# The first two weight chunks in quarters, interleaved on TensorE, and the squares of x moved from GpSimd to ScalarE and VectorE

## The chip, the cores and the metric

The kernel runs on one core of a Trainium2 chip. The metric is the device time of one launch in microseconds (us). All weights are streamed from the chip's main memory (HBM) in each launch.

## What is computed

One layer of a hybrid encoder in float32: 16 meta tokens and 256 frames (272 token columns), model width 2048. Only the front of it matters here:

```python
u = rmsnorm(h, norm_mix_g)                 # y = x * rsqrt(mean(x*x) + eps) * g
proj = u @ w_in                            # one combined input projection
rq, rk, rv, rg, cq, ckv, kr = jnp.split(proj, IN_SPLITS, axis=-1)
c_kv = rmsnorm(ckv, kv_norm_g)             # 256 wide
c_q = rmsnorm(cq, q_norm_g)                # 512 wide
# retention heads and latent attention, then
h = h + jnp.concatenate([ret_out, mla_out], axis=-1) @ w_o
h = h + jnp.square(jax.nn.relu(rmsnorm(h, norm_mlp_g) @ w_up)) @ w_down
return rmsnorm(h[frames], final_norm_g)
```

The kernel multiplies the projection weights with x times its gain first, and applies the row factor rsqrt(mean(x*x) + eps) to the results later. So the sum of squares of x is not needed by the first multiplications, but by what follows them.

## The kernel before, in words

**Layout.** Activations are transposed: 128 features on the partitions, tokens in the free dimension. x is `x_in`, 16 tiles (index k) of 128x272. Weights come in chunks: a chunk `c` is 128 output columns of a weight matrix with all 2048 input rows, stored as 128x2048 (16 tiles of 128x128, 1024 KB). Chunks 0 and 1 are the 256 columns of `ckv`, chunks 2 to 5 are `cq`, chunk 6 the rotary key, then come the heads' chunks.

**Split operands.** TensorE multiplies in a rounded float32 format (`fp32r`). To keep float32 precision each operand is split into a rounded part and a rest. For a chunk, ScalarE copies `raw` into `hi` (`split_hi`, L548, in two halves of 128x1024), and VectorE subtracts, `lo = raw - hi` (`split_lo`, L830). For x, ScalarE writes `xs[:, k, 0:TOK]`, x times gain rounded (`x_round`, L589), and VectorE writes the rest `xs[:, k, TOK:]` (`x_rest`, L843), one instruction for each of the 16 tiles on each engine. `narrow` (L323) then makes three matmuls of 272 columns for each k (lo with x, hi with the rest of x, hi with x); `wide` (L291) makes two for each k (512 and 256 columns).

**Buffers.** There are four `raw` buffers, but two of `hi`, two of `lo` and two result banks `acc`, all indexed by c % 2. A chunk's half of `hi` can be written only when the chunk two before has used that half (`chunk_used`), a chunk's matmuls can begin only when the result of the chunk two before has been read out of its bank (`acc_read`), and a load into `raw` waits until VectorE has made `lo` from it (`lo_ready`).

**Order of work.** Every engine runs its own list of instructions strictly in the order in which the code writes them, with semaphores between the engines. The start is:

- SyncE's queue (L243 to L256) issues the gains, half of chunk 0, x tiles 0 to 3, x tiles 4 to 7, the other half of chunk 0, x tiles 8 to 11 and 12 to 15, chunks 1 and 2, the constants, chunk 3, and then the stream of chunks.
- ScalarE (L584 to L605): first half of chunk 0, x tiles 0 to 7, second half of chunk 0, x tiles 8 to 15, chunk 1, chunks 2 and 3, then `kv_sq`, the squares of `ckv`.
- VectorE (L849 to L867) follows with the rests in the same order; after the splits of chunk 2 it reads the result of chunk 0 (`ckv[:, 0]`, L864), after those of chunk 3 the result of chunk 1.
- GpSimd (L1205 to L1214) waits for all of x, squares it in one instruction (`x_sq = x_in * x_in`, 128x4352) and folds the 16 tiles in halves, 8, 4, 2 and 1 tiles, counting on `ssx`.
- TensorE (L426 to L436): `narrow(0)`, tile by tile as `x_lo` allows, `narrow(1)`, `wide(2)`, `wide(3)`, then a multiplication with ones that adds the squares over the partitions (`ps_x`, L432; waits for `ssx` 5), the same for `ckv` (`ps_v`), then chunks 4, 5, 6 and the heads.

Of the kernel before, what the change touches and what calls it, by code (L numbers as in the profile page):

```python
# [13 lines left out]
P = 128  # L26
# [39 lines left out]


# [27 lines left out]
side_landed first_half gains_landed consts_landed table_in""".split()  # L95


def hymba_block(nc, w_in, w_side, w_o, w_up, w_down, x_all, x_frames, gains_in, consts_in, out):
    ctx = ExitStack()
    with ctx:  # L100
        sem = {n: ctx.enter_context(nc.semaphore(n)) for n in EVENTS}
        raw_landed = [ctx.enter_context(nc.semaphore(f"raw_landed{i}")) for i in range(RAWS)]
        x_part = [ctx.enter_context(nc.semaphore(f"x_part{i}")) for i in range(4)]
# [133 lines left out]
        def _(sp):  # L237
# [49 lines left out]
        def _(pe):  # L287
# [34 lines left out]

            def narrow(c, more=0, ready=None):  # L323
                a = acc[c % 2][:, 0:TOK]
                for k in range(KT):
                    if k % 8 == 0:
                        pe.wait_ge(sem["lo_ready"], 2 * c + k // 8 + 1 + 2 * more)
                    if k == 0 and c >= 2:
# [3 lines left out]
                    wh = hi[c % 2][:, k * P:k * P + P]  # L332
                    wl = lo[c % 2][:, k * P:k * P + P]
                    mm(a, wl, xs[:, k, 0:TOK], k == 0, False)
                    mm(a, wh, xs[:, k, TOK:], False, False)
                    m = mm(a, wh, xs[:, k, 0:TOK], False, k == KT - 1)
                    if k % 8 == 7:
                        m.then_inc(sem["chunk_used"], 1)

# [83 lines left out]
            def x_parts(k):  # L423
                pe.wait_ge(sem["x_lo"], k + 1)

            narrow(0, ready=x_parts)  # L426
            narrow(1)
# [3 lines left out]
            pe.wait_ge(sem["ssx"], 5)  # L431
# [112 lines left out]
        def _(act):  # L544
# [3 lines left out]
            def split_hi(c, part, more=0):  # L548

                if c < 0 or c >= C_END:  # L550
                    return
                if c == 0 and part == 0:
                    act.wait_ge(sem["first_half"], 16)
                elif part == 0 or c == 0:
                    act.wait_ge(raw_landed[c % RAWS], 16 * (c // RAWS + 1) + 4 * more)
                if c >= 2:
                    act.wait_ge(sem["chunk_used"], 2 * (c - 2) + part + 1 + 2 * more)
# [25 lines left out]

            act.wait_ge(sem["meta_pad"], 2)  # L584
            copy(cen[:], pt_m[:]).then_inc(sem["table_in"], 1)
            split_hi(0, 0)
            act.wait_ge(sem["gains_landed"], 16)

            def x_round(k):  # L589
                act.wait_ge(x_part[k // 4], 16)  # L590
                act.activation(xs[:, k, 0:TOK], x_in[:, k, :], ACT.Identity, scale=gain(G_MIX + k)).then_inc(sem["x_hi"], 1)  # L591

            for k in range(8):
                x_round(k)
            split_hi(0, 1)
            for k in range(8, 16):
                x_round(k)
            split_hi(1, 0)
            split_hi(1, 1)

            for c in range(2):
                split_hi(c + 2, 0)
                split_hi(c + 2, 1)
# [222 lines left out]
        def _(dve):  # L826
# [22 lines left out]
            split_lo(0, 0)  # L849
            dve.wait_ge(sem["gains_landed"], 16)  # L850
            for k in range(8):
                if k % 4 == 0:
                    dve.wait_ge(x_part[k // 4], 16)
                x_rest(k)
            split_lo(0, 1)
            for k in range(8, 16):
                x_rest(k)
            split_lo(1, 0)
            split_lo(1, 1)
            for c in range(2):  # L860
                split_lo(c + 2, 0)
                split_lo(c + 2, 1)
                dve.wait_ge(sem["chunk_used"], 2 * c + 2)
                dve.tensor_copy(ckv[:, c, :], acc[c % 2][:, 0:TOK]).then_inc(sem["acc_read"], 1)  # L864

# [329 lines left out]
        def _(pool):  # L1195
# [213 lines left out]
```

## Time and profile before

| | us |
|---|---|
| median of 3 runs | 1194.45 (1194.44 to 1195.57) |
| span of the profiled execution, first to last instruction | 1192.3 |
| TensorE busy (matmul) | 1152.4 (97%) |
| VectorE busy | 736.5 (62%) |
| ScalarE busy | 609.2 (51%) |
| GpSimd busy | 154.3 (13%) |
| mean granted TensorE clock | 0.986 of full speed |

The profiled execution gives no time of its own besides its span; the median of the runs lies 2.15 us above that span, which is what lies around the first and the last instruction. The engines are called PE (TensorE's matmuls), PEld (its weight loads), DVE (VectorE), ACT (ScalarE), POOL (GpSimd) and SP (SyncE); a "q" behind a name is the engine's sequencer, which issues DMAs. "L591" is line 591 of the kernel. All positions are us from the span's start. The busy shares are averages over 1192 us; the span in 40 slices shows TensorE at 2 tenths in the first slice, at 9 in nearly all others, and at 5 in the last one.

### The profile page before, as it was taken

The numbers are of one execution on the slowest core, as the hardware profiler recorded it, in microseconds if no ns is written. First come the engines' busy times: TensorE is split into PE (matmuls) and PEld (weight loads), VectorE is DVE, ScalarE is ACT, GpSimd is POOL, SyncE is SP. The second block draws the span as 40 slices with busy tenths as digits, with TensorE's granted clock in tenths as the row PEclk, the third lists the DMA queues.
The fourth block names the chain that finished last, engine by engine and source line by source line (L and its number), as shares of the span: only waits on it lengthen the run. The fifth ranks groups of instructions, "written<-read, shape, count | busy, mean of one in ns | idle before, by whom it ended". The sixth has DMA issues, their size and how long they took to land.

```text
span 1192.3 us, 18902 instructions
## 1 busy us (share of the span) xinstructions
PE 1152.4 (97%) x6758; PEld 1004.7 (84%) x6758; DVE 736.5 (62%) x962; ACT 609.2 (51%) x942; POOL 154.3 (13%) x167
## 2 busy tenths in 40 slices
PE   2999999999998999999999999999999999999995
PEld 2897898888887888888888888888888888888884
DVE  7786767677768667666665444445666665444443
ACT  4454565555556556555554444444555554444441
POOL 5011111111113331000000111111000000111111
PEclk7999999999999999999999999999999999999997
DMA  7443433333415554554555555455455445544531
GB/s 295 183 163 133 168 133 132 132 145 128 167 71 216 190 193 176 187 200 177 182 201 180 177 199 187 176 184 198 183 177 200 185 177 189 198 176 180 204 109 70
DMA packets 29260, 206.33 MB, mean 173 GB/s; under 512 B 3376, under 2 KB 3376, under 8 KB 5680
## 3 DMA queue, kind: packets, MB, share of 16 engines
q1 hardware_dynamic: 28080, 199.66, 46.4%
q10 hardware_dynamic: 1152, 6.29, 1.4%
q8 instruction: 18, 0.29, 0.1%
q14 instruction: 10, 0.08, 0.0%
HBM read 203.84 MB, written 2.10 MB: 173 GB/s over the span
## 4 chain that ended last, share of the span: by engine, by line
PE 95%; DVE 3%; ACT 1%; DMA 1%; issue 0%; DVEq 0%; SPq 0%; ACTq 0%
PE acc L289 86%; PE ps_qn L289 3%; PE ps_qr L289 2%; DVE xs L845 1%; PE ps_y L289 1%; PE ps_v L289 1%; PE ps_x L289 1%; PE ps_kn L289 1%; DMA x_in<-x_all 1%; DVE res L828 0%; DVE lo L828 0%; ACT xs L591 0%; DVE hid L1089 0%; DVE mla_o L828 0%; ACT hi L546 0%
## 5 line engine op out<-in xcount | busy, mean ns | idle before, releaser
L828 DVE TENSOR_TENSOR lo<-raw,hi 128x1024 fp32r<-128x1024 f32 x366 | 450.3, 1231 | 245.0 <-ACT hi L546 240.7
L289 PE MATMUL acc<-xs,hi 128*128 128x512 f32 (+1 forms) x1952 | 589.3, 365 | 0.0
L546 ACT ACTIVATE hi<-raw 128x1024 fp32r<-128x1024 f32 x366 | 386.6, 1057 | 234.5 <-PE acc L289 228.4
L289 PE MATMUL acc<-xs,lo 128*128 128x256 f32 (+1 forms) x1648 | 457.9, 286 | 22.2 <-DVE xs L845 22.2
L289 PE MATMUL acc<-hid,hi 128*128 128x512 f32 x1280 | 450.8, 400 | 3.2 <-DVE hid L1089 3.2
L289 PEld LDWEIGHTS acc<-xs,hi 128*128 128x128 f32 x1952 | 346.7, 190 | 51.6
L289 PE MATMUL acc<-hid,lo 128*128 128x256 f32 x1280 | 352.3, 281 | 0.0
L289 PEld LDWEIGHTS acc<-xs,lo 128*128 128x128 f32 x1648 | 312.3, 190 | 31.3 <-DVE lo L828 9.1
L289 PEld LDWEIGHTS acc<-hid,hi 128*128 128x128 f32 x1280 | 238.1, 189 | 59.5 <-DVE hid L1089 4.5
L289 PEld LDWEIGHTS acc<-hid,lo 128*128 128x128 f32 x1280 | 242.5, 189 | 4.7
L546 ACT ACTIVATE half_b<-acc 128x256 f32<-128x256 f32 x132 | 50.7, 384 | 216.7 <-PE acc L289 216.7
L1197 POOL TENSOR_TENSOR t<-half_b,res 128x256 f32<-128x256 f32 x47 | 34.7, 739 | 658.1 <-ACT half_b L546 650.3
L828 DVE TENSOR_TENSOR res<-acc,t 128x256 f32 (+1 forms) x47 | 20.0, 425 | 90.6 <-POOL t L1197 90.6
L828 DVE TENSOR_TENSOR z<-acc,half_b 128x256 f32<-128x256 f32 x64 | 27.2, 425 | 54.6 <-ACT half_b L546 54.6
L1197 POOL TENSOR_TENSOR sum_sq<-sum_sq,sq 128x256 f32<-128x256 f32 x47 | 51.8, 1102 | 56.1 <-ACT sq L810 36.8
L1148 DVE SCALAR_TENSOR_TENSOR r<-z,rstd 128x256 f32<-128x256 f32 x64 | 27.3, 426 | 2.2
L788 ACT ACTIVATE sq<-r 128x256 f32<-128x256 f32 x64 | 26.8, 418 | 3.3 <-DVE r L1148 3.1
L828 DVE TENSOR_TENSOR hid<-sq,hid 128x256 f32 (+1 forms) x64 | 26.9, 420 | 0.0
L789 ACT ACTIVATE hid<-r 128x256 f32 (+1 forms) x64 | 25.7, 402 | 0.0
L810 ACT ACTIVATE sq<-res 128x256 f32 (+1 forms) x32 | 13.5, 421 | 21.1 <-DVE res L828 21.1
L845 DVE SCALAR_TENSOR_TENSOR xs<-x_in,gains,xs 128x272 fp32r<-128x272 f32 x16 | 22.3, 1464 | 0.2 <-ACT xs L591 0.2
L1197 POOL TENSOR_TENSOR rk<-zk,consts 128x272 f32<-128x272 f32 x8 | 8.3, 1034 | 65.9 <-ACT swk L546 65.9
(175 smaller groups left out, 621.0 us busy)
## 6 DMA issues: line engine op xcount, KB each, us to landing
raw<-w_up SPq DMA_DIRECT2D x64, 1024.0 KB, 4.8
raw<-w_down SPq DMA_DIRECT2D x64, 1024.0 KB, 4.8
raw<-w_in SPq DMA_DIRECT2D x38, 1024.0 KB, 4.8
raw<-w_o SPq DMA_DIRECT2D x16, 1024.0 KB, 4.8
side<-w_side ACTq DMA_DIRECT2D x8, 768.0 KB, 5.8
x_in<-x_all SPq DMA_DIRECT2D x4, 544.0 KB, 7.7
res<-x_frames SPq DMA_DIRECT2D x1, 2048.0 KB, 7.6
out<-res SPq DMA_DIRECT2D x2, 640.0 KB, 3.0
```

Source lines behind the costliest of these rows:

```text
L289: return pe.matmul(o, l, m, start=start, stop=stop)
L546: return act.activation(o, i, ACT.Copy)
L788: act.activation(sq[:], r[:], ACT.Square).then_inc(sem["up_sq"], 1)
L789: act.activation(hid[:, n, 0:FRAMES], r[:], ACT.Square).then_inc(sem["up_hi"], 1)
L810: act.activation(sq[:], res[:, n, :], ACT.Square).then_inc(sem["dn_sq"], 1)
L828: return dve.tensor_tensor(o, a, b, op)
L845: dve.scalar_tensor_tensor(out=xs[:, k, TOK:], in0=x_in[:, k, :], scalar=gain(G_MIX + k), in1=xs[:, k, 0:TOK].bitcast(F32), op0=ALU.mult, ...
L1148: dve.scalar_tensor_tensor(out=r[:], in0=z[:], scalar=0.0, in1=rstd[:], op0=ALU.max, op1=ALU.mult).then_inc(sem["up_r"], 1)
L1197: return pool.tensor_tensor(o, a, b, op)
```

## The change

- SyncE's queue: the first two chunks come as quarter, quarter, half, and x in five parts (tiles 0-1, 2-3, 4-7, 8-11, 12-15), interleaved. The gains go through ScalarE's queue. The constants are issued after chunk 3 and no longer before it.
- ScalarE and VectorE split in the order in which the pieces come. ScalarE then also squares x, in four instructions of four tiles (128x1088), two after the first half of chunk 2 and two after its second half.
- VectorE folds the squares (8, 4, 2, 1 tiles: 2176, 1088, 544 and 272 columns) between the splits of chunk 3 and the reads of `ckv`. GpSimd does neither.
- TensorE multiplies tiles 0-3 of chunk 0, tiles 0-3 of chunk 1, tiles 4-7 of chunk 0, tiles 4-7 of chunk 1, then the second half of chunk 0 and that of chunk 1. The number of matmuls is the same.

```diff
+X_PARTS = ((0, 2), (2, 4), (4, 8), (8, 12), (12, 16))
+QUARTER = W // 4
@@ block.sync
-            sp.dma_start(gains[:], gains_in).then_inc(sem["gains_landed"], 16)
-            sp.dma_start(raw[0][:, 0:W // 2], w_in[0, :, 0:W // 2]).then_inc(sem["first_half"], 16)
-            sp.dma_start(x_in[:, 0:4, :], x_all[:, 0:4, :]).then_inc(x_part[0], 16)
-            sp.dma_start(x_in[:, 4:8, :], x_all[:, 4:8, :]).then_inc(x_part[1], 16)
-            sp.dma_start(raw[0][:, W // 2:], w_in[0, :, W // 2:]).then_inc(raw_landed[0], 16)
-            for n in range(2, 4):
-                sp.dma_start(x_in[:, 4 * n:4 * n + 4, :], x_all[:, 4 * n:4 * n + 4, :]).then_inc(x_part[n], 16)
-            load(w_in[1], 1)
+            piece(0, 0, 1, sem["w_0a"])      # columns [a, b) * QUARTER of chunk c
+            x_load(0)
+            x_load(1)
+            piece(1, 0, 1, sem["w_1a"])
+            piece(0, 1, 2, sem["w_0b"])
+            x_load(2)
+            piece(1, 1, 2, sem["w_1b"])
+            x_load(3)
+            piece(0, 2, 4, raw_landed[0])
+            x_load(4)
+            piece(1, 2, 4, raw_landed[1])
             load(w_in[2], 2)
+            load(w_in[3], 3)
             sp.dma_start(consts[:], consts_in).then_inc(sem["consts_landed"], 16)
-            load(w_in[3], 3)
@@ block.tensor
+            def first_pair():
+                for part in range(2):
+                    for c in range(2):
+                        pe.wait_ge(sem["part_lo"], 2 * part + c + 1)
+                        for k in range(4 * part, 4 * part + 4):
+                            if c == 0:
+                                pe.wait_ge(sem["x_lo"], k + 1)
+                            m = narrow_step(c, k)
+                        if part == 1 and c == 0:
+                            m.then_inc(sem["chunk_used"], 1)
+                for c in range(2):
+                    pe.wait_ge(sem["lo_ready"], 2 * c + 2)
+                    for k in range(8, KT):
+                        if c == 0:
+                            pe.wait_ge(sem["x_lo"], k + 1)
+                        m = narrow_step(c, k)
+                        if c == 1 and k == 8:
+                            m.then_inc(sem["chunk_used"], 1)
+                    m.then_inc(sem["chunk_used"], 1)
-            narrow(0, ready=x_parts)
-            narrow(1)
+            first_pair()
             wide(2, 2, x_wide, x_hi)
             wide(3, 3, x_wide, x_hi)
             pe.wait_ge(sem["consts_landed"], 16)
-            pe.wait_ge(sem["ssx"], 5)
+            pe.wait_ge(sem["ssx"], 8)
@@ block.scalar
+            act.dma_start(gains[:], gains_in).then_inc(sem["gains_landed"], 16)
+            def x_square(n):
+                act.activation(x_sq[:, 4 * n:4 * n + 4, :], x_in[:, 4 * n:4 * n + 4, :],
+                               ACT.Square).then_inc(sem["ssx"], 1)
+            piece_hi(0, 0, 1, sem["w_0a"]).then_inc(sem["part_hi"], 1)
             act.wait_ge(sem["gains_landed"], 16)
+            x_round(0)
+            x_round(1)
+            piece_hi(1, 0, 1, sem["w_1a"]).then_inc(sem["part_hi"], 1)
+            piece_hi(0, 1, 2, sem["w_0b"]).then_inc(sem["part_hi"], 1)
+            x_round(2)
+            piece_hi(1, 1, 2, sem["w_1b"]).then_inc(sem["part_hi"], 1)
+            x_round(3)
+            piece_hi(0, 2, 4, raw_landed[0]).then_inc(sem["hi_ready"], 2)
+            x_round(4)
+            piece_hi(1, 2, 4, raw_landed[1]).then_inc(sem["hi_ready"], 2)
+
+            split_hi(2, 0)
+            x_square(0)
+            x_square(1)
+            split_hi(2, 1)
+            x_square(2)
+            x_square(3)
+            split_hi(3, 0)
+            split_hi(3, 1)
             act.wait_ge(sem["acc_read"], C_CQ)
             act.activation(kv_sq[:], ckv[:], ACT.Square).then_inc(sem["kv_sq"], 1)
@@ block.vector
+            def x_sum(n, step):
+                dve.wait_ge(sem["ssx"], step)
+                tt(x_sq[:, 0:n, :], x_sq[:, 0:n, :], x_sq[:, n:2 * n, :], ALU.add).then_inc(sem["ssx"], 1)
+            def kv_read(c):
                 dve.wait_ge(sem["chunk_used"], 2 * c + 2)
                 dve.tensor_copy(ckv[:, c, :], acc[c % 2][:, 0:TOK]).then_inc(sem["acc_read"], 1)
...
+            piece_lo(0, 2, 4, "hi_ready", 2).then_inc(sem["lo_ready"], 2)
+            x_rests(4)
+            piece_lo(1, 2, 4, "hi_ready", 4).then_inc(sem["lo_ready"], 2)
+
+            split_lo(2, 0)
+            split_lo(2, 1)
+            kv_read(0)
+            x_sum(8, 4)
+            split_lo(3, 0)
+            split_lo(3, 1)
+            x_sum(4, 5)
+            kv_read(1)
+            x_sum(2, 6)
+            x_sum(1, 7)
@@ block.gpsimd
-            for n in range(4):
-                pool.wait_ge(x_part[n], 16)
-            tt(x_sq[:], x_in[:], x_in[:], ALU.mult).then_inc(sem["ssx"], 1)
-            n = KT // 2
-            step = 1
-            while n:
-                pool.wait_ge(sem["ssx"], step)
-                tt(x_sq[:, 0:n, :], x_sq[:, 0:n, :], x_sq[:, n:2 * n, :], ALU.add).then_inc(sem["ssx"], 1)
-                n //= 2
-                step += 1
```

The rests on VectorE before `piece_lo(0, 2, 4, ...)` follow the pieces of ScalarE one by one. `narrow_step(c, k)` is the body of the loop of `narrow`.

## Rows read from the trace of the kernel before

**Rows 1.** Chain that ended last, in order of time: start us, us, engine, what.

```profile
13.44 16.68 DVE xs L845 x4
...
30.17 14.93 PE acc L289 x93
```

**Rows 2.** Waits in the first 35 us: who waited for whom, us, times, longest.

```profile
PE acc L289 <- DVE xs L845: 22.2, 5, 9.2
```

**Rows 3.** Timeline of VectorE, 8 to 33 us: start us, us, instruction, count.

```profile
8.51 3.39 DVE L845 SCALAR_TENSOR_TENSOR xs<-x_in,gains,xs 128x272 fp32r<-128x272 f32 x8 [0.18 <-ACT xs L591]
...
13.36 7.68 DVE L845 SCALAR_TENSOR_TENSOR xs<-x_in,gains,xs 128x272 fp32r<-128x272 f32 x1
...
13.36 18.91 DVE L845 SCALAR_TENSOR_TENSOR xs<-x_in,gains,xs 128x272 fp32r<-128x272 f32 x8
```

**Rows 4.** Timeline of GpSimd, 13 to 33 us.

```profile
13.24 7.50 POOL L1197 TENSOR_TENSOR x_sq<-x_in 128x4352 f32<-128x4352 f32 x1 [11.55 <-DMA x_in<-x_all]
20.82 9.92 POOL L1197 TENSOR_TENSOR x_sq<-x_sq 128x2176 f32<-128x2176 f32 x4
```

**Rows 5.** Whole core, stretches: PE, PEld, DVE, ACT, POOL busy; PEclk, DMA share, GB/s.

```profile
26.00:33.00 7.00, 4.92 (x17) 4.09 (x18) 7.00 (x7) 0.00 (x0) 4.58 (x3) 0.50 0.00 0
...
368.00:370.00 2.00, 1.97 (x5) 1.54 (x6) 2.00 (x6) 1.36 (x2) 0.00 (x0) 0.50 0.98 418
```

**Rows 6.** Timeline of TensorE from 39 to 52 us: first matmul of chunk 2, the square sums.

```profile
39.92 0.28 PE L289 MATMUL acc<-xs,lo 128*128 128x256 f32 x1
...
50.90 0.62 PE L289 MATMUL ps_x<-x_sq,consts 128*128 128x272 f32 x2
```

**Rows 7.** Timeline: where ScalarE and GpSimd begin on what has landed.

```profile
6.02 1.06 ACT L546 ACTIVATE hi<-raw 128x1024 fp32r<-128x1024 f32 x1 [3.56 <-DMA raw<-w_in]
...
7.83 3.41 ACT L591 ACTIVATE xs<-x_in,gains 128x272 fp32r<-128x272 f32 x8 [0.76 <-DMA x_in<-x_all]
...
15.60 2.00 ACT L546 ACTIVATE hi<-raw 128x1024 fp32r<-128x1024 f32 x2
18.09 1.06 ACT L546 ACTIVATE hi<-raw 128x1024 fp32r<-128x1024 f32 x1 [0.49 <-DMA raw<-w_in]
```

**Rows 8.** Stretches of SyncE: us, PEclk, DMA share, GB/s.

```profile
3.00:4.00 1.00, 1.00 0.99 193
...
14.00:16.00 2.00, 1.00 1.02 426
```

**Rows 9.** DMA issues in the first 35 us: what, KB each, median us to landing.

```profile
x_in<-x_all SPq DMA_DIRECT2D x4, 544.0 KB, 7.7
...
gains<-gains_in SPq DMA_DIRECT2D x1, 35.0 KB, 1.9
```

**Rows 10.** ScalarE's squares of ckv, from the timeline.

```profile
42.58 0.66 ACT L605 ACTIVATE kv_sq<-ckv 128x544 f32<-128x544 f32 x1 [1.64 <-DVE ckv L864]
```

**Rows 11.** VectorE's groups by form, 35 to 110 us: count, busy us, mean ns, idle before.

```profile
L828 DVE TENSOR_TENSOR lo<-raw,hi 128x1024 fp32r<-128x1024 f32 x22 | 26.8, 1221 | 6.4 <-ACT hi L546 6.4
L828 DVE TENSOR_TENSOR side_lo<-side,side_hi 128x1280 fp32r<-128x1280 f32 x2 | 3.0, 1492 | 3.4 <-ACT side_hi L546 3.4
L864 DVE COPY ckv<-acc 128x272 f32<-128x272 f32 x2 | 0.9, 434 | 0.0
```

**Rows 12.** TensorE alone, stretches: us, busy, PEclk, DMA share, GB/s.

```profile
14.05:21.20 7.15, 0.01 (x1) 0.65 1.01 421
...
33.30:50.90 17.60, 17.60 (x116) 1.00 0.56 209
```

**Rows 13.** Timeline of TensorE: first matmul of neighbouring k-steps of chunk 0, at two rates.

```profile
9.97 0.43 PE L289 MATMUL acc<-xs,lo 128*128 128x272 f32 x1
...
10.65 0.43 PE L289 MATMUL acc<-xs,lo 128*128 128x272 f32 x1
...
33.30 0.29 PE L289 MATMUL acc<-xs,lo 128*128 128x272 f32 x1
...
33.67 0.29 PE L289 MATMUL acc<-xs,lo 128*128 128x272 f32 x1
```

More of the change, by code:

```diff
@@ L102, in hymba_block @@
         raw_landed = [ctx.enter_context(nc.semaphore(f"raw_landed{i}")) for i in range(RAWS)]
-        x_part = [ctx.enter_context(nc.semaphore(f"x_part{i}")) for i in range(4)]
+        x_part = [ctx.enter_context(nc.semaphore(f"x_part{i}")) for i in range(len(X_PARTS))]
         at = (nc.sbuf_base + 31) // 32 * 32
@@ L327, in narrow @@
                         pe.wait_ge(sem["lo_ready"], 2 * c + k // 8 + 1 + 2 * more)
[L328 removed]
+                    if k == 0:
                         pe.wait_ge(sem["acc_read"], c - 1 + more)
@@ L548, in split_hi @@
             def split_hi(c, part, more=0):
-                if c < 0 or c >= C_END:
+                if c >= C_END:
                     return
-                if c == 0 and part == 0:
-                    act.wait_ge(sem["first_half"], 16)
-                elif part == 0 or c == 0:
+                if part == 0:
                     act.wait_ge(raw_landed[c % RAWS], 16 * (c // RAWS + 1) + 4 * more)
-                if c >= 2:
-                    act.wait_ge(sem["chunk_used"], 2 * (c - 2) + part + 1 + 2 * more)
+                act.wait_ge(sem["chunk_used"], 2 * (c - 2) + part + 1 + 2 * more)
                 copy(halves(hi, c, part), raw_half(c, part)).then_inc(sem["hi_ready"], 1)
@@ L580, in side_split, with piece_hi, x_round @@
                 copy(side_hi[:], side[:, 0:SIDE_V]).then_inc(sem["side_hi"], 1)
+            act.dma_start(gains[:], gains_in).then_inc(sem["gains_landed"], 16)
             act.wait_ge(sem["meta_pad"], 2)
             copy(cen[:], pt_m[:]).then_inc(sem["table_in"], 1)
-            split_hi(0, 0)
-            act.wait_ge(sem["gains_landed"], 16)
[L589 to L603, printed above, removed]
+            def piece_hi(c, a, b, landed):
+                act.wait_ge(landed, 16)
+                return copy(hi[c][:, a * QUARTER:b * QUARTER], raw[c][:, a * QUARTER:b * QUARTER])
+            def x_round(n):
+                act.wait_ge(x_part[n], 16)
+                for k in range(*X_PARTS[n]):
+                    act.activation(xs[:, k, 0:TOK], x_in[:, k, :], ACT.Identity,
+                                   scale=gain(G_MIX + k)).then_inc(sem["x_hi"], 1)
+            def x_square(n):
+                act.activation(x_sq[:, 4 * n:4 * n + 4, :], x_in[:, 4 * n:4 * n + 4, :],
+                               ACT.Square).then_inc(sem["ssx"], 1)
+            piece_hi(0, 0, 1, sem["w_0a"]).then_inc(sem["part_hi"], 1)
+            act.wait_ge(sem["gains_landed"], 16)
+            x_round(0)
[16 more added lines that the diff above has]
+            split_hi(3, 1)
             act.wait_ge(sem["acc_read"], C_CQ)
@@ L847, in x_rest, with piece_lo, x_rests @@
                                          op1=ALU.subtract).then_inc(sem["x_lo"], 1)
[L849 to L862, printed above, removed]
+            def piece_lo(c, a, b, done, count):
+                dve.wait_ge(sem[done], count)
+                q = slice(a * QUARTER, b * QUARTER)
+                return tt(lo[c][:, q], raw[c][:, q], hi[c][:, q].bitcast(F32), ALU.subtract)
+            def x_rests(n):
+                for k in range(*X_PARTS[n]):
+                    x_rest(k)
+            def x_sum(n, step):
+                dve.wait_ge(sem["ssx"], step)
+                tt(x_sq[:, 0:n, :], x_sq[:, 0:n, :], x_sq[:, n:2 * n, :], ALU.add).then_inc(sem["ssx"], 1)
+            def kv_read(c):
                 dve.wait_ge(sem["chunk_used"], 2 * c + 2)
                 dve.tensor_copy(ckv[:, c, :], acc[c % 2][:, 0:TOK]).then_inc(sem["acc_read"], 1)
+            piece_lo(0, 0, 1, "part_hi", 1).then_inc(sem["part_lo"], 1)
+            dve.wait_ge(sem["gains_landed"], 16)
+            x_rests(0)
+            x_rests(1)
+            piece_lo(1, 0, 1, "part_hi", 2).then_inc(sem["part_lo"], 1)
+            piece_lo(0, 1, 2, "part_hi", 3).then_inc(sem["part_lo"], 1)
+            x_rests(2)
+            piece_lo(1, 1, 2, "part_hi", 4).then_inc(sem["part_lo"], 1)
+            x_rests(3)
+            piece_lo(0, 2, 4, "hi_ready", 2).then_inc(sem["lo_ready"], 2)
[11 more added lines that the diff above has]
+            x_sum(1, 7)
             dve.wait_ge(sem["kv_sq"], 1)
```

25 lines of the change are left out of this document (16 added, 9 removed).

## The prediction

> **What bounds the kernel now.** I read the chain that ended last first. Over the whole span it is matmuls almost throughout, so only a change that removes TensorE's idle time can pay. In the front of the span one piece is not matmuls: four rests of x on VectorE take 16.68 us of the chain [rows 1]. The waits say the same from the other side: TensorE waited 22.2 us, five times, for the rests of x [rows 2]. Next the timeline of VectorE. The first eight rests take 3.39 us together, one every 0.41 us. The second eight, the same instruction on the same shape, take 18.91 us, and the first of those alone 7.68 us [rows 3]. The timeline of GpSimd lies beside it: its squaring starts at 13.24 us and takes 7.50 us, the four folds end at 30.74 us [rows 4]. The first slow rest starts 0.12 us after the squaring and ends 0.3 us after it. It isn't the transfers that slow VectorE: from 26 to 33 us none runs, and VectorE is still busy for all 7 us with only seven instructions [rows 5]. So GpSimd's reads hold up VectorE's instructions with two SBUF inputs, these hold up TensorE, and the whole stream behind waits.
>
> From 33.3 us on TensorE has no gap until the square sums. The first matmul of chunk 2 starts at 39.92 us and the sum of x's squares (`ps_x`) at 50.90 us, so a wide chunk takes (50.90 - 39.92) / 2 = 5.49 us [rows 6]. After that the code is untouched and bound by TensorE, so I carry the shift of `ps_x` to the end of the kernel one to one. My sum is therefore one number: when does `ps_x` start in the changed kernel, against 50.90 us.
>
> **Landings.** Before, the front half of chunk 0 is there at 6.02 us, the first x part at 7.83, chunk 1 at 15.60 and chunk 2 at 18.09 us, by the starts of ScalarE on them [rows 7]; so 1024 KB take 2.5 us, 544 KB take 1.33, 512 KB 1.25, 272 KB 0.66, 256 KB 0.62. The queue is full: 426 GB/s at a DMA share of 1.02 [rows 8]. The changed queue brings the same bytes up to the end of chunk 1, in another order. The gains leave this queue (0.44 us sooner), the rows in HBM get shorter, and in the first microseconds the DMA engines are busy (share 0.99) at only 193 GB/s [rows 8], which short rows could make worse. I let the first gain be eaten up and take 15.7 us for the last piece of chunk 1. Backwards: x tiles 12-15 at 14.45, second half of chunk 0 at 13.1, x 8-11 at 11.85, chunk 1's second quarter 10.5, x 4-7 at 9.9, chunk 0's second quarter 8.6, chunk 1's first quarter 7.95, x 2-3 at 7.3, x 0-1 at 6.65, the first quarter near 5. Forwards: chunk 2 at 18.2, chunk 3 at 20.7, the constants near 23.8 us, long before `ps_x` needs them. Bounds: 0.4 us earlier (the gains' issue), 2.5 us later: the first four short pieces are 1056 KB, which take 2.6 us at 426 GB/s and 5.6 at the 193 GB/s of the first microseconds; that is 3.0 more, some of which the landings before already hold.
>
> **A rule that speaks against this.** The Trainium skill (DMA: Bandwidth & Descriptors, Anatomy of one DMA) puts some 2.0 us of fixed time on each DMA beside its bytes, and under Bandwidth asks to batch to 1 MiB or more. The page measured DMAs issued by GpSimd, these are SyncE's. It is priced as a rival below.
>
> **ScalarE.** A rounding of an x tile costs 3.41 / 8 = 0.41 to 0.43 us, a half chunk 0.94 to 1.06 [rows 7]. The squares are new. The nearest row is the square of 128x544, 0.66 us [rows 10]; a copy of 128x1024 is 1.06 us [rows 7]; on the line through both, 128x1088 is 1.11 us, four are 4.4 us. No table load stands before that square, so I add none. From the last rows that wait for data: x 8-11 to 13.5 us, second half of chunk 0 to 14.5, x 12-15 to 16.2, second half of chunk 1 to 17.2, then a wait for chunk 2 (18.2), its first half to 19.2, two squares to 21.4, its second half to 22.4, two squares to 24.7, chunk 3's halves to 25.7 and 26.7 us.
>
> **VectorE.** With GpSimd silent I take the undisturbed times: a rest 0.41 us [rows 3], a half chunk 1.22, a read of `ckv` 0.43 us [rows 11]. A fold of 2176 columns is on no row; from 1221 ns at 1024 and 1492 at 1280 columns [rows 11] the slope is 1.06 ns a column, hence 2.4, 1.3, 0.7 and 0.4 us for the four folds. The first two folds, 3.7 us, are the ones on the path; their lower bound is the 3.7 us less 0.5 (the pitch in a row of instructions is shorter than the duration), the upper 1.5 us more, if two inputs from one buffer slowed them as no row shows. Then: rests 8-11 by 14.2, the second half of chunk 0's `lo` by 15.8, rests 12-15 by 17.9, chunk 1's by 19.1, chunk 2's first half 20.4, its second half (waits for ScalarE's 22.4) 23.7, read of chunk 0's result 24.1, first fold (waits for the last square, 24.7) 27.1, chunk 3's halves 28.3 and 29.4, second fold 30.7, read of chunk 1's result 31.2, last folds 32.3 us.
>
> **TensorE.** A k-step of a narrow chunk takes 10.65 - 9.97 = 0.68 us at the low rate and 33.67 - 33.30 = 0.37 us at the high one [rows 13]. Tiles 0-7 of both chunks need 16 steps, 5.9 us (10.9 at the low rate), and have from about 7.5 to 15.8 us. Interleaving gives TensorE work while the rests come at 0.41 us, but none of that sets the end: chunk 0's last steps wait for the rests (17.9), chunk 1's second half for its `lo` (19.1) and ends at 19.1 + 8 x 0.37 = 22.1 us. Now the new waits: chunk 2 may begin only when chunk 0's result is read. That read stands behind chunk 2's second split, which stands behind two squares on ScalarE: 24.1 us, 2.0 us idle. Chunk 2 ends at 29.6. Chunk 3 waits for the read of chunk 1's result, queued behind two folds: 31.2 us, 1.6 us idle. It ends at 31.2 + 5.5 = 36.7, `ps_x` starts at 36.8 us (folds are done at 32.3). The gain is 50.9 - 36.8 = 14.1 us. The squares and folds that GpSimd did beside the others thus cost 3.6 us on the path now, the release of VectorE gives 15.5 (18.91 - 3.39), and the rest, some 2 us, is TensorE's work pulled forward and run at the high rate.
>
> **Queues passed.** The gains on ScalarE's queue delay its first copies by one issue (0.4 us), while it waits for data anyway. Four more issues on SyncE, some 0.5 to 0.7 us each, run while the queue is full. GpSimd's next duty is after chunk 5. Chunks 4 and 5 can be loaded once `lo` of chunks 0 and 1 is made (15.8, 19.1 us) and queue behind the constants: there by 29 us, needed after 37.
>
> **The clock.** The granted clock falls to 0.65 and 0.50 while TensorE idles from 14 to 21 us, and is 1.00 again from 33.3 us [rows 12], after it worked without a gap from 30.17 us [rows 1]. In the changed kernel it works with short gaps from 7 us. Even if the low rate lasted to 20 us, chunk 1's second half would end at 24 us, when the read of 24.1 us binds anyway: no cost. Further on, TensorE waits for the last rests before the output projection and the clock falls to 0.50 at 368 us for 2 us or more [rows 5]; that may fall out otherwise by 1 us either way.
>
> **Result.** The span was 1192.3 us, so 1178.2; the median of the runs lies 2.15 us above: 1180.4 us.
>
> **Rivals.**
> - *The clock stays low longer.* With the low rate to 31 us, chunks 0 and 1 end at 16.3 + 16 x 0.68 = 27.2, chunk 2 gets 5.8 of its 16 steps done by 31 and ends at 34.6, `ps_x` starts at 40.2 us: 1183.8. Up to 1187 if it lasts through chunk 3's start. For it: the waits of 2.0 and 1.6 us. Against it: before, about 3 us of unbroken work brought the clock up. 6%.
> - *Each DMA has a fixed cost in line.* The gains, 35 KB, take 1.9 us to land, four x parts of 544 KB 7.7 us each [rows 9], yet they were issued some 0.5 us apart and land 1.33 us apart: the fixed part overlaps. If it didn't, four more DMAs would cost 4 x 1.9 = 7.6 us, all on the chain from chunk 1 on: 1188. 3%. This is what the skill's 2.0 us would come to here.
> - *GpSimd isn't what slows VectorE,* and the eight late rests take 18.9 us as before. Then `ps_x` starts near 50 us and the time is 1194. Against it stand [rows 3 to 5]. 3%.
> - *Slower: the low clock lasts past the front.* If the new gaps keep TensorE at the low rate, chunks 2 and 3 take 5.5 x 0.68 / 0.37 = 10.1 us each: 27.2, 37.3, 47.4 us, still 3.5 us ahead; every further microsecond at the low rate loses 0.46, so it turns slower if the low rate lasts past 55 us, and by the end of chunk 5 (69 us against 63) the kernel is 6 us slower: 1200. No row shows half rate under gapless work for longer than about 4 us. 2%.
> - The rest, 2%, is more gain than the range allows.
>
> **How the numbers follow.** The forecast holds 84%. Its range: landings -0.4 to +2.5 us, folds and squares -0.5 to +1.5, clock at 368 us 1 either way, spread of the runs 1.1 upwards; not all at once, so 1178.3 to 1184.5 us. That takes in the nearer part of the first rival. A measurement of this kernel can tell about 0.2% (2.4 us) from no change. Faster by more: 84 + 6 + 3 + 2 = 95%. Within: 3%. Slower: 2%.
>
> **What the profile will show.** All rests of x near 0.5 us each; `x_sq` on ScalarE at about 1.1 us, folds at 2.4 and 1.3 us; chunk 1's last piece read by ScalarE at or after 15.7 us; TensorE idle about 2 us before chunk 2 and 1.6 us before chunk 3, waiting for the copies into `ckv`; `ps_x` near 37 us; the distance from `ps_x` to the end as before, within 1 us. I would be wrong if that distance grows, if the pieces land late, or if a rest stays long.

## The result and the profile after

The changed kernel takes 1180.49 us (1179.91 to 1180.91, 4 runs) against 1194.95 us of the kernel before in the same rounds: a ratio of 0.9877, 95% interval 0.9864 to 0.989. Its profiled execution has a span of 1178.5 us; that run's time was 1180.24. In a second comparison (`e13`) it was 1180.09 us, ratio 0.9876 (0.9859 to 0.9892).

The page of the profile after, the head and the busy times:

```profile
span 1178.5 us, 18915 instructions
...
PE 1150.6 (98%) x6758; PEld 1003.5 (85%) x6758; DVE 725.4 (62%) x968; ACT 612.8 (52%) x948; POOL 136.4 (12%) x162
```

TensorE does the same 6758 matmuls; GpSimd lost 18 us of work. The chain that ended last in the first 50 us, in order of time (start us, us, what), answers [rows 1]:

```profile
6.64 12.01 DMA raw<-w_in
...
18.67 1.06 ACT hi L569
19.73 0.50 ACT x_sq L619
...
20.64 1.09 ACT x_sq L619
21.73 0.95 ACT hi L569
22.68 2.00 ACT x_sq L619 x2
...
24.71 2.42 DVE x_sq L867
27.13 2.27 DVE lo L867 x2
29.40 1.20 DVE x_sq L867
30.60 0.36 DVE ckv L903
...
31.10 5.86 PE acc L292 x32
```

The 16.68 us of rests are gone from it. In their place stands what the change put in: from 18.67 to 30.96 us the chain runs through the squares, the folds and the read of `ckv`. Groups by form in the first 36 us, rests, squares and the two large folds (count, busy us, mean ns, idle before) answer [rows 3]:

```profile
L884 DVE SCALAR_TENSOR_TENSOR xs<-x_in,gains,xs 128x272 fp32r<-128x272 f32 x16 | 6.9, 496 | 0.9 <-ACT xs L615 0.8
L619 ACT ACTIVATE x_sq<-x_in 128x1088 f32<-128x1088 f32 x4 | 4.2, 1093 | 0.0
L867 DVE TENSOR_TENSOR x_sq<-x_sq 128x2176 f32<-128x2176 f32 x1 | 2.4, 2425 | 0.4 <-ACT x_sq L619 0.4
L867 DVE TENSOR_TENSOR x_sq<-x_sq 128x1088 f32<-128x1088 f32 x1 | 1.3, 1283 | 0.0
```

All 16 rests take 496 ns on the mean, where the mean before was pulled up to 1464 ns. TensorE's timeline holds two waits between chunk 1 and `ps_x`:

```profile
24.43 0.47 PE L292 MATMUL acc<-xs,hi 128*128 128x512 f32 x1 [1.62 <-DVE ckv L903]
...
31.10 0.47 PE L292 MATMUL acc<-xs,hi 128*128 128x512 f32 x1 [0.82 <-DVE ckv L903]
...
36.80 0.62 PE L292 MATMUL ps_x<-x_sq,consts 128*128 128x272 f32 x2
```

`ps_x` starts at 36.80 us where it started at 50.90 [rows 6]. From there to the end of the span it is 1141.7 us, and 1141.4 before (1192.3 - 50.9): the whole gain is made in the first 37 us.

### The profile page after: what moved, and what is told of

It reads as the page before. It is cut to its first block, busy times and chain, and to the rows that moved or that the text cites. A ratio compares the mean times of both kernels' runs of the same rounds, so it can differ in the third digit from the quotient of the medians.

```text
span 1178.5 us, 18915 instructions
## 1 busy us (share of the span) xinstructions
PE 1150.6 (98%) x6758; PEld 1003.5 (85%) x6758; DVE 725.4 (62%) x968; ACT 612.8 (52%) x948; POOL 136.4 (12%) x162
## 4 chain that ended last, share of the span: by engine, by line
PE 94%; DVE 2%; DMA 1%; ACT 1%; SPq 0%; issue 0%; DVEq 0%
PE acc L292 86%; PE ps_qn L292 3%; PE ps_qr L292 2%; PE ps_y L292 1%; PE ps_v L292 1%; DMA raw<-w_in 1%; PE ps_x L292 1%; PE ps_kn L292 1%; DVE res L867 0%; DVE lo L867 0%; DVE x_sq L867 0%; ACT x_sq L619 0%; DVE hid L1152 0%; ACT hi L569 0%; DVE mla_o L867 0%
## 5 line engine op out<-in xcount | busy, mean ns | idle before, releaser
L867 DVE TENSOR_TENSOR lo<-raw,hi 128x1024 fp32r<-128x1024 f32 (+1 forms) x368 | 450.6, 1225 | 242.4 <-ACT hi L569 238.0
L569 ACT ACTIVATE hi<-raw 128x1024 fp32r<-128x1024 f32 (+1 forms) x368 | 387.0, 1052 | 214.4 <-PE acc L292 208.8
L1260 POOL TENSOR_TENSOR sum_sq<-sum_sq,t 128x256 f32<-128x256 f32 x8 | 5.9, 738 | 78.0 <-ACT t L715 78.0
```

The costliest lines, as they stand in the source:

```text
L569: return act.activation(o, i, ACT.Copy)
L867: return dve.tensor_tensor(o, a, b, op)
L1260: return pool.tensor_tensor(o, a, b, op)
```

## Experiments

In each of them two numbers are read: the median against the kernel before in the same rounds, and the start of `ps_x` in the profile, which is free of what happens later. One place behind `ps_x` matters to the comparison: before the output projection TensorE waits and the clock falls, and it stays low for a time that differs. The mean granted clock from 340 to 380 us is 0.96 in the kernels before and after, and 0.91 in `e1`, `e4`, `e5`, `e6` and `e10`. Behind `ps_x`, `e1`, `e5` and `e6` take 1142.4 to 1142.5 us instead of the 1141.4 to 1141.9 of `before`, the changed kernel and `e3`, so this place is worth some 0.8 us. `e4` and `e10` also wait elsewhere. The stretch in the changed kernel (us, TensorE busy, PEclk, DMA share, GB/s) and in `e1`:

```profile
340.00:380.00 40.00, 36.62 (x195) 0.96 0.53 189
```

```profile
340.00:380.00 40.00, 36.78 (x190) 0.91 0.50 186
```

**What held VectorE up.** `e5`: the kernel before, GpSimd squares one tile.

```diff
-            tt(x_sq[:], x_in[:], x_in[:], ALU.mult).then_inc(sem["ssx"], 1)
-            n = KT // 2
...
-                tt(x_sq[:, 0:n, :], x_sq[:, 0:n, :], x_sq[:, n:2 * n, :], ALU.add).then_inc(sem["ssx"], 1)
+            tt(x_sq[:, 0, :], x_in[:, 0, :], x_in[:, 0, :], ALU.mult).then_inc(sem["ssx"], 1)
```

> The kernel before with its pieces and order; GpSimd squares only tile 0 of x (272 columns) and folds nothing, so the row factor is computed from a sixteenth of the squares. It prices what GpSimd's squares and folds cost by holding up VectorE, with nothing put in their place. Theory A: all 16 rests take about 0.5 us each but for one beside the short square, chunk 2 starts near 23.5, ps_x near 34.5 us, 1178.2 us; less 1180.5 for the changed kernel, this leaves the squares' new place costing more than the quarters bring. Theory B (the quarters are needed for the gain): 1181 us or more.

Measured: 1179.63 us, ratio 0.9868 (0.9852 to 0.9885), `ps_x` at 35.66 us. The eight late rests take 3.77 us together, not 18.91. That is 15.2 us at `ps_x`, more than the 14.1 of the whole change, with nothing but GpSimd's work gone. The one late rest that met the short square took 0.88 us. I had expected `ps_x` at 34.5; chunk 2 begins near 24.4 us and not at 23.5. Theory A held in its direction, and theory B (1181 us or more) fell.

`e6`: GpSimd kept busy for 11.3 us beside the rests, but only writing.

```diff
-            tt(x_sq[:], x_in[:], x_in[:], ALU.mult).then_inc(sem["ssx"], 1)
...
-                tt(x_sq[:, 0:n, :], x_sq[:, 0:n, :], x_sq[:, n:2 * n, :], ALU.add).then_inc(sem["ssx"], 1)
+            pool.memset(x_sq[:], 16.0).then_inc(sem["ssx"], 1)
+            for step in range(1, 3):
+                pool.wait_ge(sem["ssx"], step)
+                pool.memset(x_sq[:], 16.0).then_inc(sem["ssx"], 1)
```

> The kernel before; in place of the square and the folds GpSimd writes a constant into all of x_sq three times (128x4352, no operand read) and folds nothing, so the row factor is computed from a constant. From the small fills, 0.31 us for 256 columns, each takes near 4 us, from 13.2 to some 25 us. Theory A (what VectorE waits for is GpSimd's reading): rests stay near 0.5 us, 1178.2 us as with one square. Theory C (anything that GpSimd does to this memory holds VectorE up): the first rest is blocked for about 4 us, one rest for each fill, ps_x about 9 us later, 1187 us.

Measured: 1179.4 us, ratio 0.9865 (0.9848 to 0.9881), `ps_x` at 35.42 us. The timelines of GpSimd and VectorE:

```profile
13.34 3.75 POOL L1207 MEMSET x_sq<- 128x4352 f32 x1 [11.64 <-DMA x_in<-x_all]
17.14 7.54 POOL L1210 MEMSET x_sq<- 128x4352 f32 x2
...
13.47 3.39 DVE L845 SCALAR_TENSOR_TENSOR xs<-x_in,gains,xs 128x272 fp32r<-128x272 f32 x8
```

GpSimd is busy from 13.34 to 24.68 us without a gap, on the same buffer, and the eight rests beside it take 3.39 us, the undisturbed time. So it isn't GpSimd being at work, and not its writing: what is left is its reading of operands. That agrees with the Trainium skill (SBUF — State Buffer, Who interferes with whom), by which a VectorE instruction with two inputs in SBUF contends with a GpSimd instruction that reads SBUF, not with one that only writes it. The page calls the port pair that the two engines share an exclusive lock; the 7.68 us of [rows 3] beside the 7.50 us of [rows 4] are its number here.

That the number of VectorE's SBUF inputs matters, and who comes first, can be seen at 82 us in the trace of the kernel before, where GpSimd multiplies two operands beside VectorE:

```profile
81.82 1.22 DVE L828 TENSOR_TENSOR lo<-raw,hi 128x1024 fp32r<-128x1024 f32 x1
...
83.24 0.42 DVE L828 TENSOR_TENSOR qn<-ps_qn,qn_b 128x256 f32<-128x256 f32 x1 [0.20 <-ACT qn_b L546]
...
82.05 1.58 POOL L1197 TENSOR_TENSOR rq<-zq,consts 128x256 f32<-128x256 f32 x1 [12.14 <-DVE zq L828]
```

The split with two SBUF inputs was there first and keeps its 1.22 us; GpSimd's instruction begins 0.23 us later and ends 0.59 us after the split, at 83.63 us. The addition at 83.24 us has one input in PSUM and one in SBUF: it takes its usual 0.42 us beside GpSimd. No run shows a GpSimd instruction that reads only one operand.

`e2`: the new pieces and order, squares and folds back on GpSimd, nothing of them on ScalarE and VectorE.

> The changed kernel with the squares and folds back on GpSimd, beside VectorE. Theory A (GpSimd's reads hold up VectorE): squaring starts when the last x part has landed, near 14.5 us, the rests 12 to 15 and the half chunks after it get through one for each GpSimd instruction, the last lo of chunk 1 comes near 33 us, ps_x near 47 us, 1191 us. Theory B (the pieces themselves make the gain): ps_x near 37 us, 1180.5 us.

Measured: 1193.83 us, ratio 0.9988 (0.9979 to 0.9998), `ps_x` at 49.89 us. VectorE and GpSimd:

```profile
15.20 8.30 DVE L863 TENSOR_TENSOR lo<-raw,hi 128x1024 fp32r<-128x1024 f32 x1 [0.33 <-ACT hi L569]
23.43 10.12 DVE L880 SCALAR_TENSOR_TENSOR xs<-x_in,gains,xs 128x272 fp32r<-128x272 f32 x4
...
14.98 7.44 POOL L1252 TENSOR_TENSOR x_sq<-x_in 128x4352 f32<-128x4352 f32 x1 [13.29 <-DMA x_in<-x_all]
22.50 10.74 POOL L1252 TENSOR_TENSOR x_sq<-x_sq 128x2176 f32<-128x2176 f32 x4
```

Now the half chunk of `lo` meets the square (8.30 instead of 1.22 us), and four rests meet the four folds, one each. Alone, the quarters and the interleaving bring 1.0 us at `ps_x`. I had expected 3.9; only the direction held. One VectorE instruction gets through for each of GpSimd's (in the kernel before, rests of 7.68, 5.01, 2.72, 1.58 and 0.99 us stand beside the square and the four folds), whichever stands there, and the last is over at 33.5 us here as it was at 32.3 before.

**What the quarters and the interleaving bring.** `e1`: only the squares moved (ScalarE's and VectorE's part of the diff), pieces and order as before.

> The kernel before (halves of chunk 0, whole chunk 1, chunk after chunk on TensorE) with only the squares moved: ScalarE squares and VectorE folds in the places that the changed kernel has. Theory A (the release of VectorE is the whole gain and the read of chunk 0's result sets the start of chunk 2): the rests end at 16.8 us, chunk 1 ends at 23.1, the read of ckv is over at about 24.0, chunk 3 starts near 31.1, the sum of x's squares (ps_x) near 37 us, the median 1180.5 us, the same as the changed kernel. Theory B (the quarters and the interleaving bring the 2 us by which TensorE's work came forward): ps_x near 39 us, 1182.5 us.

Measured: 1180.59 us, ratio 0.987 (0.9854 to 0.9887), `ps_x` at 36.40 us. That is the changed kernel's time without one of its new pieces: they bring nothing where the change has them. `ps_x` is even 0.4 us earlier than in the changed kernel, which the place at 340 to 380 us takes back. Theory A held. Chunk 1 ends later (chunk 2 starts near 24.3 us without a wait), but the read of chunk 0's result lets chunk 2 begin only at 24.4 us in the changed kernel too.

`e11`: the changed kernel, but TensorE takes chunk 0 and then chunk 1.

```diff
...
+                for c in range(2):
+                    for k in range(KT):
+                        if k in (0, 4):
+                            pe.wait_ge(sem["part_lo"], k // 2 + c + 1)
+                        if k == 8:
+                            pe.wait_ge(sem["lo_ready"], 2 * c + 2)
+                        if c == 0:
+                            pe.wait_ge(sem["x_lo"], k + 1)
+                        m = narrow_step(c, k)
+                        if k % 8 == 7:
+                            m.then_inc(sem["chunk_used"], 1)
```

> The changed kernel with its pieces, squares and folds in place; only TensorE's order is that of before: all of chunk 0, then all of chunk 1. It prices the interleaving where the changed kernel has it. Theory A (chunk 1 then has all 16 steps left after the last rest, 16 x 0.37 = 5.9 us, and ends at 24.1 us where the read of ckv lets chunk 2 begin at 24.4 anyway): ps_x at 36.8 us as before, 1180.5 us. Theory B (TensorE's work pulled forward is part of the gain): 1.5 us more, 1182 us.

Measured: 1182.34 us, ratio 0.9888 (0.9871 to 0.9904), `ps_x` at 39.35 us, 2.55 us later than in the changed kernel. My theory A fell. TensorE's timeline, the two gaps and some neighbouring k-steps, first of `e11`:

```profile
11.35 0.56 PE L292 MATMUL acc<-xs,lo 128*128 128x272 f32 x1 [1.19 <-DVE xs L875]
...
16.40 0.60 PE L292 MATMUL acc<-xs,lo 128*128 128x272 f32 x1 [2.00 <-DVE lo L858]
...
21.33 0.43 PE L292 MATMUL acc<-xs,lo 128*128 128x272 f32 x1
...
22.01 0.39 PE L292 MATMUL acc<-xs,lo 128*128 128x272 f32 x1
...
22.49 0.28 PE L292 MATMUL acc<-xs,lo 128*128 128x272 f32 x1
...
22.86 0.29 PE L292 MATMUL acc<-xs,lo 128*128 128x272 f32 x1
```

and of the changed kernel:

```profile
12.68 0.43 PE L292 MATMUL acc<-xs,lo 128*128 128x272 f32 x1
...
13.33 0.29 PE L292 MATMUL acc<-xs,lo 128*128 128x272 f32 x1
...
13.71 0.29 PE L292 MATMUL acc<-xs,lo 128*128 128x272 f32 x1
```

A k-step takes 0.68 us until 22.0 us in `e11` (22.01 - 21.33), and until about 13 us in the changed kernel, and 0.37 after that (22.86 - 22.49; 13.71 - 13.33 is 0.38). With the chunks in turn TensorE idles 1.19 and 2.00 us in between, and the rate rises 9 us later. From 16.4 us on eight steps run at 0.68 instead of 0.37 us: 8 x 0.31 = 2.5 us, which is the difference. (The column of the granted clock shows 1.00 here in both. That 0.68 us is the pace of the low clock can be seen later in the kernel before: the same step took 0.68 us at 31.94 and 32.62 us, under a granted clock of 0.50.)

```profile
31.90:33.30 1.40, 1.40 (x9) 0.50 0.00 0
```

So with quarters, interleaving isn't there to do work early: it closes TensorE's gaps, and I read the late rise as the gaps' doing. No run puts in gaps alone. The moment of the rise also differs where there is no gap before it: the first step of 0.38 us or less begins at 10.8 us in `e12`, 11.3 in `e3`, 12.1 in `e9`, 12.6 in `e4`, 12.8 in `e2` and 13.3 in the changed kernel, all with a first matmul at 7.1 to 7.4 us. None of them comes near the 22.49 us of `e11`. With halves, as in `e1`, TensorE starts at 9.35 us with eight tiles at hand and has no gap before 16 us either; there the first fast step begins at 14.71 us.

**What the squares' new place costs.** `e3`: the changed kernel without them.

```diff
-            x_square(0)
-            x_square(1)
+            act.activation(x_sq[:, 0, :], x_in[:, 0, :], ACT.Square).then_inc(sem["ssx"], 1)
...
-            x_sum(1, 7)
```

> The changed kernel, of the squares of x only tile 0's is made and no fold, so that the row factor is computed from a sixteenth of the squares. It prices the squares and folds where they stand. Theory A (they are on the path through the two reads of ckv): no idle time before chunks 2 and 3, chunk 2 starts at 22.3, ps_x at 33.4 us, 1176.9 us. Theory B (they are hidden, something else delays the reads): 1180.5 us.

Measured: 1177.82 us, ratio 0.9849 (0.9832 to 0.9865), `ps_x` at 33.91 us. The waits before chunks 2 and 3 are gone, as theory A had it. Where they stand, squares and folds cost 36.80 - 33.91 = 2.9 us. And without the squares the quarters are worth something: `ps_x` is at 35.66 in `e5`, so 1.75 us. In the changed kernel the one eats up the other.

`e4`: the same squares and folds, all behind the splits of chunk 3 and the reads.

```diff
             split_hi(2, 0)
-            x_square(0)
-            x_square(1)
             split_hi(2, 1)
-            x_square(2)
-            x_square(3)
             split_hi(3, 0)
             split_hi(3, 1)
+            for n in range(4):
+                x_square(n)
...
             kv_read(0)
-            x_sum(8, 4)
             split_lo(3, 0)
             split_lo(3, 1)
-            x_sum(4, 5)
             kv_read(1)
+            x_sum(8, 4)
+            x_sum(4, 5)
             x_sum(2, 6)
             x_sum(1, 7)
```

> The changed kernel with the same squares and folds, but all four squares after ScalarE's last half of chunk 3 and all four folds after the read of chunk 1's result. Theory A (only their place costs): chunk 2 starts at 22.3 us, chunk 3 at 27.8, ps_x at 33.4, the folds end near 33 us, chunk 4 starts within 0.5 us of its turn; 1177.2 us, 3.3 below the changed kernel. Theory B (what is saved there comes back at chunk 4, whose splits and whose result bank now wait behind squares and folds): 1179.5 us or more.

Measured: 1182.01 us, ratio 0.9883 (0.9866 to 0.9899): not better than the changed kernel by 3.3 us but worse by 1.5, although `ps_x` starts at 34.18 us, 2.6 us earlier. TensorE and VectorE of `e4`:

```profile
49.38 0.36 PE L292 MATMUL acc<-xs,lo 128*128 128x272 f32 x1 [2.78 <-DVE cq L865]
...
50.40 0.43 PE L292 MATMUL acc<-xs,lo 128*128 128x272 f32 x1
...
51.08 0.43 PE L292 MATMUL acc<-xs,lo 128*128 128x272 f32 x1
...
28.18 4.99 DVE L865 TENSOR_TENSOR x_sq<-x_sq 128x2176 f32<-128x2176 f32 x4 [2.43 <-ACT x_sq L619]
...
44.48 1.85 DVE L960 RECIPROCAL kv_var<-kv_f 128x272 f32<-128x272 f32 x1 [0.59 <-ACT kv_f L657]
...
48.81 0.42 DVE L865 TENSOR_TENSOR cq<-acc,half_b 128x256 f32<-128x256 f32 x1
```

The folds now end at 33.17 us, the split of chunk 4 and the reads of `cq` follow them, then the root of the row factor, two reciprocals of 1.85 us, and only then the read of chunk 4's result at 48.81 us, for which chunk 6 waits 2.78 us. In the changed kernel that read is no later than here, and chunk 6 starts right behind chunk 5:

```profile
48.60 0.42 DVE L867 TENSOR_TENSOR cq<-acc,half_b 128x256 f32<-128x256 f32 x1
...
37.88 11.21 PE acc L292 x64
...
49.16 0.87 PE acc L292 x5
```

(the first line from VectorE's timeline, the others from the chain). The read ends at 49.02, chunk 5 at 49.09 us: VectorE has no slack there. The saved time ran into that wall, and TensorE's idle time cost a second time, since the steps of chunk 6 are again at the low rate (51.08 - 50.40 = 0.68) until 53.1 us. From `ps_x` to the end `e4` takes 1146.3 us, 4.6 more than the changed kernel. The wait is 2.78 of it; the six slow steps take 3.74 us, some 1.5 more than at 0.38 us each (my estimate); some 0.5 comes at 340 to 380 us, which begins 4.1 us later behind `ps_x` than in the changed kernel (352.11 - 34.18 against 350.65 - 36.80). Theory B held in the time; the wait came at chunk 6, for chunk 4's result.

`e9`: `e4`, and chunk 4's result read before the second reciprocal (on both engines the steps of chunk 6 moved into the wait for the root).

> The kernel with the late squares, and in addition chunk 4's result is read and chunk 6 is split while ScalarE and VectorE wait for each other over the row factor of ckv: ScalarE's first half of chunk 6 and its copy of chunk 4's bank stand before the root for ckv, VectorE's two splits of chunk 6 and the read of chunk 4's result before the reciprocal for ckv. Theory A (the late squares lost their gain because chunk 6 waits for the result of chunk 4 to be read, behind the chain over ps_x, roots and reciprocals): ps_x at 34.2 us, no wait before chunk 6, which starts near 46.5 us, 1177.7 us. Theory B (the chain comes back at a later consumer, the first projection of the latent attention): 1179.5 us or more.

Measured: 1180.34 us, ratio 0.9877 (0.986 to 0.9893), `ps_x` at 33.78 us. The wait before chunk 6 is gone and its successor is there, in the waits of 49 to 60 us:

```profile
PE ps_y L292 <- DVE cq_ss L871: 2.4, 1, 2.4
```

VectorE is busy for all 7 us from 49 to 56 us. My reading is that it has too much to do before the sum of `cq`'s squares, and that the order only picks the one who waits; in `e12` below, with less folding left behind the reads, neither wait is there. Theory B held in the time, with another consumer than it named. The four runs of `e9` lie in two groups, 1179.34 and 1179.43 against 1181.25 and 1181.42 us, so its median says little; the profile is of the faster group.

`e10`: `e9` with the halves and the order of before.

> As the run before it in this list (late squares, chunk 4's result read first), but with the pieces and the order of the kernel before: chunk 0 in halves, chunk 1 whole, chunk after chunk on TensorE. It prices quarters and interleaving where nothing behind hides them. Theory A: chunk 1's matmuls end about 1.3 us later than with quarters (23.6 against 22.3 us) and nothing behind makes it good, so 1.3 us above the quartered one. Theory B (something later absorbs it): the same time within 0.5 us.

Measured: 1181.86 us, ratio 0.9886 (0.987 to 0.9903), `ps_x` at 35.35 us, 1.57 us later than in `e9`. Theory A held: that is about the quarters' worth of `e5` against `e3`. The medians of `e9` and `e10` can't be set against each other closely, for the two groups of `e9`; the profiled execution of `e10` is its slowest (1183.49 us, the others 1181.73 to 1181.94).

`e12`: the squares in ScalarE's waits for data, the folds in four parts, one of them in VectorE's wait before chunk 2, four behind the reads. Nothing is left out.

```diff
             piece_hi(0, 1, 2, sem["w_0b"]).then_inc(sem["part_hi"], 1)
+            x_square(0)
             x_round(2)
...
             piece_hi(1, 2, 4, raw_landed[1]).then_inc(sem["hi_ready"], 2)
+            x_square(1)
             split_hi(2, 0)
-            x_square(0)
-            x_square(1)
             split_hi(2, 1)
             x_square(2)
-            x_square(3)
             split_hi(3, 0)
             split_hi(3, 1)
+            x_square(3)
...
```

> The changed kernel with the same four squares and as many columns folded, but the squares in ScalarE's waits for data (tiles 0 to 3 before the rounding of tiles 4 to 7, tiles 4 to 7 behind the last half of chunk 1, tiles 8 to 11 behind chunk 2, tiles 12 to 15 behind chunk 3) and the folds tile group by tile group: the first in VectorE's wait before chunk 2's splits, the other four behind the read of chunk 1's result. Theory A (between ps_x and chunk 6 VectorE has no slack, but 3.9 us less of folding is left after the reads than with the late squares): chunk 2 starts near 22.9, ps_x near 34.1 us, no wait before chunk 6, 1177.8 us, below every kernel that does all the work. Theory B (the chain of roots and reciprocals behind ps_x sets chunk 6 whatever the folds do): 1180 us or more.

Measured: 1177.91 us, ratio 0.9852 (0.9836 to 0.9869), `ps_x` at 34.47 us. VectorE's timeline, the reads of `ckv` and the folds:

```profile
19.12 1.29 DVE L867 TENSOR_TENSOR x_sq<-x_sq 128x1088 f32<-128x1088 f32 x1
...
22.59 0.43 DVE L905 COPY ckv<-acc 128x272 f32<-128x272 f32 x1
...
25.21 0.43 DVE L905 COPY ckv<-acc 128x272 f32<-128x272 f32 x1
25.57 4.05 DVE L867 TENSOR_TENSOR x_sq<-x_sq 128x1088 f32<-128x1088 f32 x4
...
46.26 0.42 DVE L867 TENSOR_TENSOR cq<-acc,half_b 128x256 f32<-128x256 f32 x1
```

The folds end at 29.6 instead of the 33.2 us of `e4`, and chunk 4's result is read at 46.26 instead of 48.81 us. TensorE still waits 0.42 us before chunk 2, and then not again until 62 us. Theory A held. The changed kernel and this one then stood in one comparison:

> The changed kernel itself, on the same chip and in the same rounds as the kernel with the squares in the gaps, so that the two can be set beside each other directly. Both theories: 0.9875 of the kernel before.

> The kernel with the squares in ScalarE's waits and the folds behind the reads once more, beside the changed kernel. Theory A (the 2.4 us between them are the two waits for the reads of ckv): ps_x 2.5 us earlier than in the changed kernel and 2.5 us less in the median. Theory B (the difference was that of two chips): within 0.8 us of the changed kernel.

Measured: 1180.09 us for the changed kernel (1179.72 to 1180.41), 1177.86 us for the other (1177.66 to 1178.65), ratios 0.9876 and 0.9859 (0.9843 to 0.9876); `ps_x` at 36.69 and 34.50 us. The runs of the two don't overlap: 2.2 us at both places, so theory A held, with 2.2 for the 2.5 us that it named. The kernel with the squares in the gaps beats the kernel before and the changed one, and lies as low as `e3`, which leaves the squares out.

## Why the prediction came out right, point by point

**The cause** [rows 1 to 5]: right, and shown by `e5` and `e6`. With it the rival by which GpSimd isn't what slows VectorE is out.

**The landings.** I let the last piece of chunk 1 land at 15.7 us; it was issued at 5.95 and landed 10.2 us later, at 16.15. Chunk 2 was read at 18.67 us, not at 18.2. The whole queue ran 0.45 us later than I took it, inside my bounds; before, ScalarE read chunk 2 at 18.09 us [rows 7], 0.58 us sooner. The six short pieces did not add a fixed cost each: the rival with 7.6 us is out.

**ScalarE and VectorE.** Squares 1.09 us (1.11 taken), folds 2.42 and 1.28 (2.4 and 1.3). One stretch was too short in the sum: ScalarE was busy with x tiles 4 to 7 and chunk 1's second quarter from 10.26 to 12.53 us, and so rounded x tiles 8 to 11 from 12.44 to 14.19 us, not to 13.5. The second half of chunk 0's `lo` was done at 16.46 us, not at 15.8. The reads of `ckv` ended at 24.28 and 30.95 us (24.1 and 31.2 taken).

**TensorE.** The first wait was 1.62 us, not 2.0. TensorE waited until 16.52 us for that `lo` of chunk 0 and then ran the last 16 steps of the two chunks without a gap, to 22.8 us. So chunk 1's second half didn't wait for its own `lo` (19.26 us), as I had it with an end at 22.1: TensorE reached it at 19.64. Chunk 2 began 0.3 us later than taken. The second wait was 0.82, not 1.6 us: chunk 2 began late and took 5.85 us to its end at 30.28, where the sum had 5.5.

The 5.49 us for a wide chunk was a misreading of [rows 6]. The matmul at 39.92 us is the second of chunk 2; the first, of 512 columns, is one of the three in the row before it in TensorE's timeline of the kernel before:

```profile
39.43 0.65 PE L289 MATMUL acc<-xs,hi 128*128 128x272 f32 x3
39.92 0.28 PE L289 MATMUL acc<-xs,lo 128*128 128x256 f32 x1
```

In the changed kernel chunk 3 takes 36.80 - 31.10 = 5.70 us.

`ps_x` was taken at 36.8 us and started at 36.80, and that is luck to this degree: errors cancelled. Chunk 2 landed 0.47 us late, but ScalarE's two halves and four squares took 6.0 and not 6.5 us (back to back, one starts before the one before it is over), so the first fold began at 24.71 us, as taken. From there to the end of the second read VectorE took 6.24 and not 6.5 us, chunk 3 began 0.15 us after that read, and took 5.70 and not 5.6 us to `ps_x`. The last step of the sum has such a pair too. The profiled execution's time lies 1.74 us above its span (1180.24 - 1178.5) and those of the other runs 1.7 to 1.9, so some 0.3 of the 2.15 us that I added was the spread of the runs; the span came out 0.3 us longer than my 1178.2.

**The carry to the end**: right, 1141.7 against 1141.4 us. But I called what lies behind `ps_x` bound by TensorE. That was true by a margin that I didn't look up: VectorE's read of chunk 4's result ends 0.1 us before chunk 6's turn (in the lines under `e4`). With `ps_x` 2.6 us earlier and the folds behind the reads the carry failed (`e4`); with `ps_x` 2.3 us earlier and less folding there it held (`e12`).

**What failed** is the sharing out of the gain. I put some 2 us down to "TensorE's work pulled forward and run at the high rate" and, a few lines before, wrote of the interleaving that "none of that sets the end". Both are wrong as they stand. The pieces bring nothing in the changed kernel (`e1`, at `ps_x` 0.4 us less than nothing), 1.0 us if GpSimd still squares (`e2`), 1.75 if nobody does (`e3`, `e5`). The gain is 15.2 us from the release of VectorE (`e5`) less what the squares' new place costs beyond what the pieces bring (2.9 less 1.75, so 1.1), which is the 14.1. And with quarters the interleaving does set the end: without it the low rate lasts to 22 us and costs 2.5 us (`e11`). I had argued the clock from the gaps in the changed kernel only, and never for the order that the interleaving replaces.

**The rivals.** The low clock did not last (to 13 us, not to 31), but `e11` shows that the mechanism is near: there TensorE idled 1.19 and 2.00 us in its first 9 us, and the steps stayed at 0.68 us until 22.0. The slower rival, with the low rate through chunks 2 and 3, didn't come: their steps take 0.35 us. And there was no gain beyond the range.

## What to carry to other kernels

Don't put a reading GpSimd instruction beside VectorE's instructions with two operands in SBUF: the rest that met the square wasn't slowed in proportion, it was stopped for the whole of it (7.68 beside 7.50 us). Since one instruction of VectorE got through for each of GpSimd's, several short squares should have cost less than one long one; no run here tries that. The price is read where VectorE feeds TensorE. When work is moved off an engine, look for the waits for data of the engine that takes it, and for what is queued behind it up to the next consumer; the same squares cost 2.9 us in one place, 0.6 in another (34.47 - 33.91), and in a third moved the wait 15 us down the stream. And before a gain is carried through to the end, look up how close the next engine is to being late.

## What the runs showed that I had not expected

- A fill of 128x4352 by GpSimd takes 3.75 us and disturbs VectorE's rests not at all (`e6`); a multiplication of the same size takes 7.50 us and stops them.
- From its first matmul at 7.1 us on, TensorE's rate rose at about 13 us with no gap between them, and at 22.0 us with two gaps of 1.19 and 2.00 us (`e11`). The granted clock's column says 1.00 throughout; the steps of 0.68 and 0.37 us say otherwise.
- Quarters of 256 KB, the first of them issued 0.47 us apart, cost the stream little, far from one fixed cost for each of them: the last piece of chunk 1 landed at 16.15 us, and chunk 2 was read 0.58 us later than before.
